# Two DMA queues for the first loads, and another order of VectorE's work at the layers' boundary and at the end of a decoder trunk

## The chip, the cores and the metric

One NeuronCore of a Trainium2 chip runs the whole kernel. The metric is the device time of one execution in microseconds (us). TensorE (PE) multiplies, VectorE (DVE) and ScalarE (ACT) work elementwise, GpSimd (POOL) issues indirect and small transfers, SyncE (SP) issues nearly all the others. Every engine has its own stream of instructions, and they meet at semaphores only.

## The reference

All in float32: SEQ = 512 tokens, D = 1024, two layers.

```python
for l in range(DEPTH):
    mod = silu(c) @ w_ada[l] + b_ada[l]
    sh1, sc1, g1, sh2, sc2, g2 = jnp.split(mod, 6, axis=-1)
    h = modulate(rmsnorm(x, norm1_g[l]), sh1, sc1)
    x = x + g1 * mixer(h, ...)    # projections w_in, retention, pooling, gates, w_out
    h = modulate(rmsnorm(x, norm2_g[l]), sh2, sc2)
    x = x + g2 * moe(h, ...)      # 16 experts, each token goes to two of one group
return rmsnorm(x, final_g)
```

Each expert computes `(silu(x @ w_gate) * (x @ w_up)) @ w_down` for its tokens; the two results of a token are weighted and added.

## The kernel before

The tokens lie in four tiles of 128 rows (t = 0 to 3). A float32 product is made of three passes: each operand is cut into a high part (rounded to fp32r, on ScalarE, names with `_hi`) and the rest (on VectorE, `_lo`), and `three_passes` (L1873 to L1875) multiplies low by high, high by low and high by high. The weights come as pieces of 512 KB through eight slots `raw`, which SP fills in a fixed order; ScalarE makes `w_hi` of a piece, VectorE `w_lo` (L1057 in the mixer, L1602 in the experts), and then the slot is free. The order of the work on each engine is written out by hand.

**The start.** SP loads four x tiles (`x_load`, 512 KB each), then the left column halves of four adaLN pieces (`column_half_load` part 0, 256 KB each, into `raw`), then `first_w` pieces, right halves and more. ScalarE's own queue carries `cond_raw` (4 KB) and, after the sigmoid, `first_rows` (16 KB, biases and norm weights). GpSimd loads `const` (470 KB). ScalarE computes for each x tile the sum of squares (L690) and the deviation (L696), VectorE the reciprocal and `first_normed` (L1148), behind `first_table`, which takes `first_rows` turned by TensorE (L2261, L1093). TensorE multiplies the column halves by the condition (`first_columns`, L2233), then folds, transposes x (L1973) and begins the first products. `keep_busy` (L2003) are matmuls without a use for the result; they read `ones_r`.

**The last expert and the layers' boundary.** Rows that experts 0 to 14 produced are written by indirect transfers into `y_rows` and read back as pairs for each token tile (`pair_early` for t = 0, 1, `pair_2`, `pair_3`; `pairs_load` on SP, L570 to L573). `combine(l, t)` (L1691) adds the pair's two parts, weighted, to x on VectorE, one instruction a part. For t = 2 TensorE does that with diagonal matrices (`pair_matmuls`, L2138). The last expert's rows don't pass through memory: `last_rows_out` (L1633) scales them, `last_rows(l, t)` (L2125) on TensorE spreads them over the tokens of tile t, and `last_add` (L1702) on VectorE adds that to x and raises `x_final`. ScalarE then computes the tile's deviation, VectorE `norm_tile` (h_nat, L1171 and L1173), TensorE `norm_transposes` (L1962), ScalarE hT_hi (L732), VectorE `norm_lo` (hT_lo, L1184), and TensorE takes tile t of group q (`group_tile`, 24 matmuls). The transposed tiles go through two PSUM banks, so a tile's products wait until `norm_lo` has read them (`unit_free`). `last_rows(l, 3)` of layer 0 uses the banks of tile 2 and waits until `last_add(l, 2)` has read them.

**The end.** After the last layer VectorE does combine, `last_add` and `normed_output` (L1711, L1715) tile by tile, and SP stores the tiles (L625, L629). For t = 2 TensorE also adds x itself by an identity matmul (L2389).

**The gate row.** `gate_row` holds g1 or g2, broadcast to all partitions by GpSimd's transfer (L2410); behind the routing VectorE waits for it (L1803) before expert 0. Its first reader is `rows_out(0)` (L1625), in expert 1's turn.

Of the kernel before, what the change touches and what calls it, by code (L numbers as in the profile page):

```python
# [21 lines left out]
ACT = mybir.ActivationFunctionType  # L22
# [3 lines left out]
D = 1024  # L26
T = 512
DEPTH = 2
NT = T // P
# [24 lines left out]
ADA_PIECES = 4  # L54
# [150 lines left out]
def build(nc, w, x_in, c_in, consts, rotary, ada_rows, pool_w, pool_scale, final_g, out):  # L205
# [7 lines left out]
    with ExitStack() as ctx:  # L213
# [59 lines left out]
        squares = sb("squares", [P, D], F32, B)  # L273
# [110 lines left out]
        def k(name):  # L384
            o, n = CONST_AT[name]
            return const[:, o:o + n]
# [149 lines left out]
        def _(sp):  # L536
# [40 lines left out]
                sp.sem_inc(landed[W_SLOTS + j], 16)  # L577
                first_load(PRE + stored_piece(0, W_SLOTS + j), W_SLOTS + j)

            for t in range(NT):  # L580
                x_load(t)
            for j in range(ADA_PIECES):
                column_half_load(2, j, 0, left_landed[j])
            first_w_load(0)
            for j in range(ADA_PIECES):
# [77 lines left out]
        def _(act):  # L663
            act.sem_inc(state_ready, 3)
            act.dma_start(cond_raw[:], c_in).then_inc(c_landed, 16)
            act.wait_ge(c_landed, 16)
            act.activation(cond[:], cond_raw[:], ACT.Sigmoid).then_inc(cond_sig, 1)
            act.dma_start(first_rows[:], ada_rows[0:4].rearrange("a (i p) -> (a i) p", p=P)).then_inc(first_rows_landed, 16)
            act.activation(spare[:], cond_raw[:, 0:1], ACT.Sqrt, scale=0.0)
            act.wait_ge(consts_landed, 16)  # L670
            act.activation(ones_r[:], k("ones"), ACT.Copy).then_inc(ones_ready, 1)

            def hi(l, q, r):
                if l == 0 and q < FIRST_W:
# [13 lines left out]
            def row_deviations(t):  # L688

                act.activation(squares[:], x[:, t], ACT.Square, accum_out=x_ss[:, t:t + 1])  # L690
                act.drain()
                deviation(t)
# [253 lines left out]
            def first_deviation(t):  # L946

                act.wait_ge(x_landed[t], 16)
                row_deviations(t)

            for t in range(NT):
                first_deviation(t)
# [83 lines left out]
        def _(v):  # L1036
# [554 lines left out]
            def expert(l, e):  # L1591
# [29 lines left out]

                def rows_out(before):

                    rows_ready(before)
                    v.tensor_tensor(y_out[:, before % 2].rearrange("p (h n) -> p h n", h=2), ps[:, 2:4],  # L1625
                                    gate_row[:].rearrange("p (h n) -> p h n", h=2), ALU.mult).then_inc(y_copied, 1)
# [10 lines left out]
                if last:  # L1637
                    rows_out(e - 1)
                    lo_e(next(pieces))
                    lo_e(next(pieces))  # L1640
                    last_hot(l)
                    hidden(0)
                    lo_e(next(pieces))
                    hidT(0)
                    if l < DEPTH - 1:
                        for q in range(EARLY):
                            early_low(l + 1, q)
                    lo_e(next(pieces))
                    lo_e(next(pieces))
                    hidden(1)  # L1650
                    lo_e(next(pieces))
                    hidT(1)
                    if l < DEPTH - 1:
                        v.drain().then_inc(raw_used, EARLY)
                    combine(l, 0, [0])
                    last_rows_out()
                    combine(l, 0, [1])
                else:
                    lo_e(next(pieces))
                    lo_e(next(pieces))  # L1660
                    if e == 0:
                        row_numbers(l)
                    if e:
                        rows_out(e - 1)
                    hidden(0)
                    lo_e(next(pieces))
                    lo_e(next(pieces))
                    hidT(0)
                    lo_e(next(pieces))
                    lo_e(next(pieces))  # L1670
                    hidden(1)
                    lo_e(next(pieces))
                    hidT(1)
                    lo_e(next(pieces))
                    lo_e(next(pieces))
                    gathered_lo(E + 1, 1 - odd, [0])
                    lo_e(next(pieces))
                    gathered_lo(E + 1, 1 - odd, [1])
                    for n in pieces:
                        lo_e(n)  # L1680
                    if e == 4:
                        pair_shares()
                    if e == 7:
                        pair_weights()
                    if e == 10:
                        overflow_count()
# [31 lines left out]
            for l in range(DEPTH):  # L1718
# [44 lines left out]
                else:  # L1763
# [2 lines left out]
                    combine(l - 1, 1, [1])  # L1766
                    norm_tile(l, 0, "h1", 0)
                    last_add(l - 1, 1)
                    lo(l, 2, RAW_OF_W[2])
                    norm_lo(l, "h1", 0)  # L1770
                    lo(l, 3, RAW_OF_W[3])
                    norm_tile(l, 0, "h1", 1)
                    last_add(l - 1, 2)
                    norm_lo(l, "h1", 1)
                    combine(l - 1, 3, [0])
                    norm_tile(l, 0, "h1", 2)
                    combine(l - 1, 3, [1])
                    norm_lo(l, "h1", 2)
                    last_add(l - 1, 3)
                    norm_tile(l, 0, "h1", 3)  # L1780
                    norm_lo(l, "h1", 3)
                for q in range(0 if l else W_SLOTS, LAST["O0"] + 1):
# [17 lines left out]
                v.wait_ge(parts_ready, l * 2 + 1)  # L1800
                v.tensor_copy(lg_parts[:, 0:3 * P], ps[:, 7, 0:3 * P]).then_inc(early_parts_copied, 1)
                route_tokens(l)
                v.wait_ge(gate_landed, l * 32 + 32)  # L1803
                for e in range(NE):
                    if e == NE - 1:
                        before, count = overflow_blocks(v, l)
# [61 lines left out]
        def _(pe):  # L1868
# [70 lines left out]
            def group_tile(l, g, t):  # L1939

                for j in range(GROUPS[g][1]):
                    if g == 0 and t == 1 and j == 3:
                        norm_transposes(l, t + 1)
                    if g == NGROUP - 1 and t >= 1 and j == 2:
                        x_transposes(l, t - 1)
                    if g == NGROUP - 1 and t == NT - 1 and j == 3:
                        x_transposes(l, t, [0])
                    product(l, g, j, t)
# [343 lines left out]
            for l in range(DEPTH):  # L2292

                pe.wait_ge(y_copied, l * NE + 1)
                if l:
                    last_rows_pairs(l - 1)
                    norm_transposes(l, 0)
                    last_rows(l - 1, 2)
                    for t in range(NT):
                        pe.wait_ge(unit_free, unit_value(l, "h1", 2 * t + 1) + 2)  # L2300
                        group_tile(l, 0, t)
                        if t == 0:
                            norm_transposes(l, 1)
                            last_rows(l - 1, 3)
                        if t == 2:
                            norm_transposes(l, 3)
                for g in range(1, NGROUP - 1):
                    if ORDER[l][g] == "ap1":
                        pe.wait_ge(norm_pack_landed, l * 16 + 16)
# [39 lines left out]
                with pe.If(count > 0):  # L2349
# [3 lines left out]
                    with pe.Fori(0, count) as slot:  # L2353
# [26 lines left out]
                            mm.then_inc(ov_step, 1)  # L2380
                        pe.wait_ge(ov_pair, b * 80 + 80)
                pe.nop()
                last_rows(l, 0)
                last_rows(l, 1)
                if l == DEPTH - 1:
                    last_rows_pairs(l)
                    pe.wait_ge(x_settled, 1)
                    for half in range(2):
                        pe.matmul(ps[:, ADD_BANK[l][2] + half], ident, x[:, 2, 512 * half:512 * half + 512], start=False, stop=False)  # L2389
                    last_rows(l, 2)  # L2390
                    last_rows(l, 3)
# [223 lines left out]
```

## Time and profile before

| | us |
|---|---|
| median of three runs | 1471.42 |
| lowest and highest | 1470.08, 1474.26 |
| the profiled execution, own time | 1468.83 |
| its span | 1467.2 |
| TensorE busy in it | 1432.4 |
| VectorE busy | 1137.9 |
| ScalarE busy | 775.8 |
| granted clock of TensorE | 0.999 |

The profiled execution is one more run beside the three. Its span is what all rows below refer to; 1.63 us of its own time lie outside the span. Layer 0's mixer begins near 20 us, its experts near 437; layer 1's mixer begins near 742, its experts near 1156. Matmul ends are modelled, so neighbouring matmuls overlap in the rows.

### The profile page before, as it was taken

What the parts mean: (1) busy time and instruction counts of PE and PEld (TensorE: products, weight loads), DVE (VectorE), ACT (ScalarE), POOL (GpSimd) and SP (SyncE); (2) the same over time, 40 slices, a digit from 0 to 9 for tenths busy, and PEclk for the clock granted to TensorE, in tenths of its full rate; (3) what the DMA queues carried; (4) which work ended last, traced back from release to release, by engine and by line L of the source; (5) the groups of instructions that cost most, each with busy time, mean ns of one, the idle gap of its engine ahead of it and who ended that gap; (6) DMA issues with size and microseconds to landing.
All of it is one profiled execution on the core that took longest, in us unless ns stands there. A gap on an engine that the chain in (4) does not pass through costs nothing.

```text
span 1467.2 us, 18889 instructions
## 1 busy us (share of the span) xinstructions
PE 1432.4 (98%) x6815; PEld 1153.5 (79%) x6815; DVE 1137.9 (78%) x1559; ACT 775.8 (53%) x1114; POOL 147.2 (10%) x138
## 2 busy tenths in 40 slices
PE   6999999999999999999989999999999999999997
PEld 4888877878878878888668887878888788888784
DVE  4885786455679999999978557854355899999998
ACT  5524424222348787777633434331233588777773
POOL 0000001000012212111100000100000122112100
PEclk9999999999999999999999999999999999999999
DMA  8766546455567999999945634633254879999995
GB/s 329 282 219 197 185 158 216 154 163 186 174 245 295 393 373 390 383 382 371 361 185 202 201 116 132 206 123 101 76 175 152 320 289 390 376 382 394 367 373 221
DMA packets 108897, 375.39 MB, mean 256 GB/s; under 512 B 16577, under 2 KB 18849, under 8 KB 108160
## 3 DMA queue, kind: packets, MB, share of 16 engines
q1 hardware_dynamic: 92464, 331.39, 62.2%
q0 software_dynamic: 15056, 38.53, 7.3%
q10 hardware_dynamic: 1280, 4.22, 0.9%
q8 instruction: 56, 0.92, 0.2%
q14 instruction: 41, 0.34, 0.1%
HBM read 361.31 MB, written 32.55 MB: 268 GB/s over the span
## 4 chain that ended last, share of the span: by engine, by line
PE 78%; DVE 14%; DMA 3%; ACT 2%; issue 2%; DVEq 1%; ACTq 0%; POOLq 0%; POOL 0%
PE ps L1873 23%; PE ps L1875 23%; PE ps L1874 23%; DVE w_lo L1602 4%; DVE w_lo_more L1602 3%; PE ps L1962 2%; DMA raw<-w 1%; PE ps L2157 1%; DVE y_out L1625 1%; PE ps L2045 1%; PE ps L2206 1%; DVE xgT_lo L1588 1%; ACT w_hi L868 1%; PE ps L2049 1%; ACT w_hi_more L868 1%
## 5 line engine op out<-in xcount | busy, mean ns | idle before, releaser
L1057 DVE TENSOR_TENSOR w_lo<-raw,w_hi 128x1024 fp32r<-128x1024 f32 x130 | 158.9, 1224 | 201.2 <-ACT w_hi L679 199.7
L679 ACT ACTIVATE w_hi<-raw 128x1024 fp32r<-128x1024 f32 x130 | 136.7, 1058 | 324.4 <-PE ps L1875 320.4
L1602 DVE TENSOR_TENSOR w_lo<-raw,w_hi 128x1024 fp32r<-128x1024 f32 x184 | 217.0, 1216 | 2.4 <-DMA gate_row<-mod_rows 1.2
L1602 DVE TENSOR_TENSOR w_lo_more<-raw,w_hi_more 128x1024 fp32r<-128x1024 f32 x176 | 207.6, 1215 | 1.3 <-ACT w_hi_more L868 0.4
L1873 PE MATMUL ps<-w_hi,hT_lo 128*128 128x512 f32 x512 | 204.3, 399 | 2.5 <-DVE hT_lo L1184 2.4
L1875 PE MATMUL ps<-w_hi,hT_hi 128*128 128x512 f32 x512 | 199.8, 390 | 0.0
L1874 PE MATMUL ps<-w_lo,hT_hi 128*128 128x512 f32 x512 | 199.4, 390 | 0.0
L868 ACT ACTIVATE w_hi<-raw 128x1024 fp32r<-128x1024 f32 x184 | 187.7, 1058 | 11.8 <-DMA raw<-w 7.4
L868 ACT ACTIVATE w_hi_more<-raw 128x1024 fp32r<-128x1024 f32 x176 | 179.1, 1057 | 9.4 <-DMA raw<-w 6.8
L1873 PE MATMUL ps<-hT_hi,w_lo 128*128 128x512 f32 x320 | 131.1, 410 | 0.7 <-DVE hT_lo L1153 0.7
L1875 PE MATMUL ps<-hT_hi,w_hi 128*128 128x512 f32 x320 | 125.0, 391 | 0.0
L1874 PE MATMUL ps<-hT_lo,w_hi 128*128 128x512 f32 x320 | 124.8, 390 | 0.0
L1873 PEld LDWEIGHTS ps<-w_hi,hT_lo 128*128 128x128 f32 x512 | 96.1, 188 | 26.2 <-DVE hT_lo L1184 4.6
L1875 PEld LDWEIGHTS ps<-w_hi,hT_hi 128*128 128x128 f32 x512 | 96.1, 188 | 20.7
L1873 PE MATMUL ps<-w_hi,xgT_lo 128*128 128x512 f32 x280 | 111.1, 397 | 0.2 <-DVE w_lo L1602 0.2
L1874 PEld LDWEIGHTS ps<-w_lo,hT_hi 128*128 128x128 f32 x512 | 96.3, 188 | 18.5
L1074 DVE SCALAR_TENSOR_TENSOR ada_acc<-raw,cond,ada_acc 128x512 f32<-128x512 f32 x140 | 104.8, 749 | 6.7 <-issue 0.4
L1875 PE MATMUL ps<-w_hi,xgT_hi 128*128 128x512 f32 x280 | 109.3, 390 | 0.0
L1874 PE MATMUL ps<-w_lo,xgT_hi 128*128 128x512 f32 x280 | 109.2, 390 | 0.0
L2427 POOL DMA_INDIRECT y_rows<-y_out,idx x30 | 65.1, 2171 | 426.8 <-DVE y_out L1625 410.1
L1873 PE MATMUL ps<-w_hi_more,xgT_lo 128*128 128x512 f32 x232 | 91.6, 395 | 0.0
L1875 PE MATMUL ps<-w_hi_more,xgT_hi 128*128 128x512 f32 x232 | 90.5, 390 | 0.0
(306 smaller groups left out, 2641.6 us busy)
## 6 DMA issues: line engine op xcount, KB each, us to landing
raw<-w SPq DMA_DIRECT2D x584, 512.0 KB, 6.1
h_rows<-h POOLq DMA_DIRECT2D x8, 1024.0 KB, 4.9
ahead<-w SPq DMA_DIRECT2D x4, 2048.0 KB, 11.8
y_rows<-x_in ACTq DMA_DIRECT2D x4, 1024.0 KB, 11.6
pair_early<-y_rows SPq DMA_DIRECT2D x4, 1024.0 KB, 6.4
x<-x_in SPq DMA_DIRECT2D x4, 512.0 KB, 6.3
raw<-w SPq DMA_DIRECT2D x8, 256.0 KB, 8.5
first_w<-w SPq DMA_DIRECT2D x4, 512.0 KB, 10.6
```

The costliest lines, as they stand in the source:

```text
L679: act.activation(w_hi[:, q % W_SLOTS], stream_piece(l, q, r), ACT.Copy).then_inc(w_hi_ready, 1)
L868: act.activation(ring_hi(r), expert_piece(e, n), ACT.Copy).then_inc(w_hi_ready, 1)
L1057: v.tensor_tensor(w_lo[:, q % W_SLOTS], stream_piece(l, q, r), w_hi[:, q % W_SLOTS], ALU.subtract).then_inc(raw_used, 1)
L1074: one = v.scalar_tensor_tensor(ada_acc[:, acc], piece, c, ada_acc[:, acc], ALU.mult, ALU.add)
L1588: v.tensor_tensor(xgT_lo[:, slot, cols], ps[:, 4 + j], xgT_hi[:, slot, cols], ALU.subtract).then_inc(xgT_lo_ready, 1)
L1602: v.tensor_tensor(ring_lo(e * EXP + n), expert_piece(e, n), ring_hi(e * EXP + n), ALU.subtract).then_inc(raw_used, 1)
L1625: v.tensor_tensor(y_out[:, before % 2].rearrange("p (h n) -> p h n", h=2), ps[:, 2:4], gate_row[:].rearrange("p (h n) -> p h n", h=2), ALU ...
L1873: pe.matmul(dst, a_lo, b_hi, start=start, stop=False)
L1874: pe.matmul(dst, a_hi, b_lo, start=False, stop=False)
L1875: return pe.matmul(dst, a_hi, b_hi, start=False, stop=stop)
L1962: one = pe.transpose(bank[:, i * P:(i + 1) * P], src[:, i * P:(i + 1) * P], ident)
L2427: pool.indirect_dma_start(y_rows, bass.IndirectOffsetOnAxis(ap=idx[:, e:e + 1], axis=0), y_out[:, e % 2], None, bounds_check=2 * T - 1, oo ...
```

## The change

Half of the first x tiles (t = 1, 3) and half of the left column halves (j = 1, 3) are issued from ScalarE's queue, right behind `cond_raw`. ScalarE waits for `const` after the first tile's squares, and makes `ones_r` after the first deviation. In the last expert both parts of `combine(l, 0)` stand before `last_rows_out`; before, one part stood behind it. At the boundary `norm_lo` of tile 0 goes ahead of `lo(2)`, `combine(3, [0])` ahead of `norm_lo` of tile 1, and `last_add(3)` ahead of `norm_lo` of tile 2; on TensorE the transposes of tile 3 go from behind tile 2's products to before their last quarter. VectorE's wait for `gate_row` goes from before expert 0 to the first reader. At the end of the last layer TensorE waits for `pair_2` and does the first half of its pair matmuls before `last_rows(0)`; the second half stays behind `last_rows(1)`.

```diff
-            for t in range(NT):
+            for t in range(0, NT, 2):
                 x_load(t)
-            for j in range(ADA_PIECES):
+            for j in range(0, ADA_PIECES, 2):
                 column_half_load(2, j, 0, left_landed[j])
...
             act.dma_start(cond_raw[:], c_in).then_inc(c_landed, 16)
+            for t in range(1, NT, 2):
+                act.dma_start(x[:, t], x_in[:, t * D:(t + 1) * D]).then_inc(x_landed[t], 16)
+            for j in range(1, ADA_PIECES, 2):
+                act.dma_start(raw[:, j].rearrange("p (i n) -> p i n", i=2)[:, :, 0:256],
+                              w[bass.ds(ADA_PIECES * 2 + j, 1)].rearrange("o p (i n) -> (o p) i n", i=2)[:, :, 0:256]
+                              ).then_inc(left_landed[j], 16)
             act.wait_ge(c_landed, 16)
             act.activation(cond[:], cond_raw[:], ACT.Sigmoid).then_inc(cond_sig, 1)
             act.dma_start(first_rows[:], ada_rows[0:4].rearrange("a (i p) -> (a i) p", p=P)).then_inc(first_rows_landed, 16)
             act.activation(spare[:], cond_raw[:, 0:1], ACT.Sqrt, scale=0.0)
-            act.wait_ge(consts_landed, 16)
-            act.activation(ones_r[:], k("ones"), ACT.Copy).then_inc(ones_ready, 1)
...
                 act.wait_ge(x_landed[t], 16)
-                row_deviations(t)
+                act.activation(squares[:], x[:, t], ACT.Square, accum_out=x_ss[:, t:t + 1])
+                act.drain()
+                if t == 0:
+                    act.wait_ge(consts_landed, 16)
+                deviation(t)
+                if t == 0:
+                    act.activation(ones_r[:], k("ones"), ACT.Copy).then_inc(ones_ready, 1)
...
                 def rows_out(before):
 
+                    if before == 0:
+                        v.wait_ge(gate_landed, l * 32 + 32)
                     rows_ready(before)
...
-                    combine(l, 0, [0])
+                    combine(l, 0)
                     last_rows_out()
-                    combine(l, 0, [1])
...
                     last_add(l - 1, 1)
+                    norm_lo(l, "h1", 0)
                     lo(l, 2, RAW_OF_W[2])
-                    norm_lo(l, "h1", 0)
                     lo(l, 3, RAW_OF_W[3])
                     norm_tile(l, 0, "h1", 1)
                     last_add(l - 1, 2)
+                    combine(l - 1, 3, [0])
                     norm_lo(l, "h1", 1)
-                    combine(l - 1, 3, [0])
                     norm_tile(l, 0, "h1", 2)
                     combine(l - 1, 3, [1])
+                    last_add(l - 1, 3)
                     norm_lo(l, "h1", 2)
-                    last_add(l - 1, 3)
...
                 route_tokens(l)
-                v.wait_ge(gate_landed, l * 32 + 32)
...
-                    if g == 0 and t == 1 and j == 3:
+                    if g == 0 and t in (1, 2) and j == 3:
                         norm_transposes(l, t + 1)
...
                             last_rows(l - 1, 3)
-                        if t == 2:
-                            norm_transposes(l, 3)
...
+                if l == DEPTH - 1:
+                    pe.wait_ge(pair_in[2], (l + 1) * PAIR_DMAS[2])
+                    pair_matmuls(0)
                 last_rows(l, 0)
                 last_rows(l, 1)
                 if l == DEPTH - 1:
-                    last_rows_pairs(l)
+                    pair_matmuls(1)
                     pe.wait_ge(x_settled, 1)
```

## Rows read from the trace of the kernel before

**Rows 1.** The page: busy us and share by engine; DMA slices.

```profile
...
PE 1432.4 (98%) x6815; PEld 1153.5 (79%) x6815; DVE 1137.9 (78%) x1559; ACT 775.8 (53%) x1114; POOL 147.2 (10%) x138
...
DMA  8766546455567999999945634633254879999995
...
```

**Rows 2.** The chain that ended last, 0 to 20 us: start us, us, what.

```profile
...
5.57 5.39 DMA first_rows<-ada_rows
...
11.10 0.29 PE ps L2261
...
14.71 0.75 DVE x L1148
...
19.73 0.50 PE ps L1873
```

**Rows 3.** Timeline, 0 to 45 us: start, us, instruction, [idle <-releaser].

```profile
...
2.77 2.98 SPq L553 DMA_DIRECT2D raw<-w  x4
...
8.52 0.31 ACT L671 ACTIVATE ones_r<-const 128x128 fp32r<-128x128 f32 x1 [1.08 <-DMA const<-consts]
...
13.53 0.19 PEld L2233 LDWEIGHTS ps<-raw,cond_wide 128*32 128x32 f32 x4 [0.56 <-DMA raw<-w]
...
14.15 0.29 ACT L696 ACTIVATE x_std<-x_ss,const 128x1 f32<-128x1 f32 x1
...
```

**Rows 4.** Windows: stretch, busy by engine, PEclk, DMA share, GB/s.

```profile
...
3.00:4.00 1.00, 0.00 (x0) 0.00 (x0) 0.00 (x0) 0.00 (x0) 0.00 (x0) 1.00 0.69 197
4.00:5.00 1.00, 0.00 (x0) 0.00 (x0) 0.00 (x0) 0.00 (x0) 0.00 (x0) 1.00 0.93 319
...
12.00:13.00 1.00, 1.00 (x9) 0.38 (x8) 0.92 (x3) 0.93 (x4) 0.00 (x0) 1.00 1.14 393
...
```

**Rows 5.** Timeline of VectorE, 720 to 772 us, the layers' boundary.

```profile
...
726.18 1.28 DVE L1691 SCALAR_TENSOR_TENSOR x<-pair_early,w_early,x 128x1024 f32<-128x1024 f32 x1 [0.51 <-DMA pair_early<-y_rows]
728.85 1.29 DVE L1633 TENSOR_TENSOR y_out<-ps,gate_row 128x512 f32<-128x512 f32 x2 [1.39 <-PE ps L1875]
...
731.99 1.28 DVE L1691 SCALAR_TENSOR_TENSOR x<-pair_early,w_early,x 128x1024 f32<-128x1024 f32 x1 [0.66 <-issue]
...
741.23 1.28 DVE L1184 TENSOR_TENSOR hT_lo<-ps,hT_hi 128x512 fp32r<-128x512 f32 x2
...
```

**Rows 6.** Timeline of TensorE, 720 to 772 us, the layers' boundary.

```profile
...
739.10 1.09 PE L1962 MATMUL ps<-const,h_nat 128*128 128x128 f32 x8 [2.31 <-DVE h_nat L1173]
...
742.57 0.50 PE L1873 MATMUL ps<-w_hi,hT_lo 128*128 128x512 f32 x1 [0.65 <-DVE hT_lo L1184]
...
757.58 0.51 PE L1873 MATMUL ps<-w_hi,hT_lo 128*128 128x512 f32 x1 [0.18 <-DVE hT_lo L1184]
...
763.18 1.09 PE L1962 MATMUL ps<-const,h_nat 128*128 128x128 f32 x8
765.85 0.50 PE L1873 MATMUL ps<-w_hi,hT_lo 128*128 128x512 f32 x1 [1.57 <-DVE hT_lo L1184]
...
```

**Rows 7.** Timeline, all engines, 1156 to 1178 us, first expert of layer 1.

```profile
...
1161.73 2.36 DVE L1602 TENSOR_TENSOR w_lo<-raw,w_hi 128x1024 fp32r<-128x1024 f32 x2 [1.15 <-DMA gate_row<-mod_rows]
...
1163.01 0.51 PE L1873 MATMUL ps<-w_hi,xgT_lo 128*128 128x512 f32 x1 [0.23 <-DVE w_lo L1602]
...
1172.80 1.09 PE L2157 MATMUL ps<-const,xg 128*128 128x128 f32 x8 [0.61 <-DMA xg<-h_rows,idx]
...
```

**Rows 8.** Timeline, all engines, 1446 to 1468 us, the end.

```profile
...
1447.24 3.67 PE L2125 MATMUL ps<-y_out,slot_last 128*128 128x512 f32 x8 [0.87 <-DVE y_out L1633]
...
1455.90 3.60 PE L2125 MATMUL ps<-y_out,slot_last 128*128 128x512 f32 x8
...
1460.15 1.22 DVE L1702 TENSOR_TENSOR x<-ps,x 128x1024 f32<-128x1024 f32 x1
...
```

**Rows 9.** DMA issues near 1439.03 us, SP: KB each, us to landing.

```profile
...
pair<-y_rows SPq DMA_DIRECT2D x1, 1024.0 KB, 10.6
```


## The prediction

> **What bounds the kernel now.** I read the page's busy shares first, then the slices, then the chain and timelines of the three places that the diff touches. TensorE is busy for 98% of the span and its slices are full from the second one on [rows 1]. So time can only be won or lost where TensorE waits or idles: in the first 20 us, at the layers' boundary and behind the last expert. In the experts VectorE and the DMA engines are full as well, so there a stall of VectorE counts. I look at four places.
>
> **Start, before.** The chain of the first 20 us doesn't run over the x tiles. It runs over first_rows, a small load on ScalarE's queue, issued at 5.57 and landed at about 11.0 [rows 2]. TensorE's first transpose (11.10) and VectorE's first_turned wait for it, the four first_normed tiles stand behind that on VectorE (the last starts at 14.71), and then come first_part, the fold, first_scale, w_lo and hT_lo up to the first product at 19.73. Everything from 11.10 to 19.73 hangs on this landing, 8.6 us behind it. ScalarE's statistics run beside it: the fourth deviation starts at 14.15 and ends 0.29 later, just in time for the last first_normed [rows 2, 3]. The two chains are equally long, so shortening one alone wins nothing.
>
> **Start, after.** The diff puts two x tiles (2 x 512 KB) and two column halves (2 x 256 KB) on ScalarE's queue ahead of first_rows. Before, first_rows was issued when all four halves were already out (SP's four issues end at 5.75) and still landed at 11.0, ahead of the last half, for which TensorE waited until 13.53 [rows 2, 3]. It could overtake since it stood in another queue. After, it stands in the same queue behind 1.5 MB. The other half of the work, also 1.5 MB, is on SP's queue, and the bandwidth is used up: 319 GB/s in the microsecond from 4 on and 393 in that from 12 [rows 4]. So I expect the halves to land about when they do now and first_rows with the last of them. What two queues may win is the low rate of the first microseconds: 197 GB/s in the one from 3 to 4 us [rows 4], and about as little in the one before; filling two or three such slices up to 400 would bring some 0.4 MB, 1.0 us at the rate of later. That leaves 12.4 to 13.4 for the landing. I take 12.9, nearer to the end that the rows show: 1.9 us later than now. Bounds: 0 (it lands as now, at 11.0) and, if SP's first_w piece (512 KB, 1.3 us at 393) also goes ahead, +3.7. The move of consts_landed lets ScalarE begin its squares before const has landed; its deviations come about 1.0 us earlier (it waited 1.08 for const before ones_r, whose 0.31 us now stand between tile 0 and 1) [rows 3]. That is hidden: VectorE waits for first_rows. ones_r itself is wanted only by keep_busy behind the columns at about 14.5. The four issues on ScalarE (at most 0.75 us each, as SP's halves [rows 3]) are over by about 4 us, and it waits for c_in until it issues first_rows at 5.57 [rows 2]: nothing. **Start: +1.9.**
>
> Here the Trainium skill bears, DMA: Bandwidth & Descriptors, "Queues, rings and completion order": engines alternate between queues packet by packet, and one queue's descriptors are consumed in order. The overtaking above agrees with the first part (11.0 against 13.4); no run here yet shows the second for a long queue. By it first_rows can't pass the halves in its own queue, so 13.4 and +2.4 would be the value, against 0 if order did not matter.
>
> **Boundary, tile 0.** Last expert of layer 0: both halves of combine(0) now go before last_rows_out. VectorE started the first at 726.18, so two of them (2 x 1.3 us) just end when the y_out multiplication starts at 728.85, and that is not delayed [rows 5]. Behind it one combine (1.3) is gone: the next combine starts at about 730.9 instead of 731.99, 1.1 earlier [rows 5]. It, last_add(0), ScalarE's squares and norm_tile(0) follow at unchanged distances, so norm_transposes(0) go from 739.10 to 738.0 [rows 6]. Now the order: before, norm_lo(0) stood behind lo(2) and started at 741.23, and the tile's product at 742.57 [rows 5, 6]. After, norm_lo(0) can run as soon as ScalarE's hT_hi is there. For tile 3 that order stood already: 2.67 us from the start of the transposes at 763.18 to the product at 765.85 [rows 6]. So here 738.0 + 2.6 = 740.6. TensorE itself is through its transposes and last_rows(2) (0.9 + 1.8) at 740.7. So the product starts at 740.7: 1.9 earlier. lo(2) now ends at 741.7; its piece is needed 12 matmuls (2.7 us) into the tile, at 743.4. Hidden by those; if it stood another 1.7 later it would not be.
>
> **Boundary, tiles 1 to 3.** Walking on with 5.5 us a tile (24 matmuls; tile 2 took 5.6 from 757.58 to 763.18), 0.9 for eight transposes, 1.8 for one last_rows (half of 3.60) [rows 6, 8] and VectorE's durations of before: VectorE's norm_tile(1) ends at 745.5, tile 0 ends at 746.2, last_rows(3) at 748.9. norm_lo(1) now stands behind combine(3,[0]) and ends at 749.3: tile 1 starts at 749.3, about 1.4 earlier, some of the lead gone. Tile 2 starts at 756.1 by the same steps, against 757.58 [rows 6]. Then the moved transposes: before, norm_transposes(3) came behind tile 2 at 763.18, and TensorE waited for hT_lo until 765.85, 2.67 us with 0.9 of work in them [rows 6]. After, they stand before the last quarter of tile 2, at 756.1 + 4.1 = 760.2. Is h ready? last_add(3) is moved ahead of norm_lo(2) and ends at 754.8, ScalarE's deviation at 756.6 (squares start behind hT_hi at 755.2), norm_tile(3) takes 2.8: 759.6. Yes, with 0.6 to spare. hT_lo is there at 760.2 + 2.7 = 762.9, TensorE's own work ends at 762.5. Tile 3 starts at 762.9 instead of 765.85 [rows 6]: **boundary −2.9**, −2 if the 0.6 and the distances of norm_lo(2) don't hold, −3.4 if TensorE doesn't wait at tile 3. All that comes later is started by TensorE's and VectorE's own progress, so it moves along.
>
> **The gate wait.** In layer 1 VectorE stood 1.15 us for gate_row before expert 0's w_lo at 1161.73. Behind it TensorE waited at 1163.01 (0.23) and, because the row numbers and so the gathers were late, at 1172.80 (0.61) [rows 7]. gate_row is read first by expert 1's turn, some 20 us on, so the new wait costs nothing. In layer 0 no such wait stands: 0. **−0.8**, the sum of TensorE's two waits; bounds 0 and −1.15.
>
> **The end.** pair_matmuls(0) now go before last_rows(0), with a wait for pair_2. TensorE was idle for 0.87 us before last_rows at 1447.24, but pair_2 was issued at 1439.03 and landed 10.6 later, at 1449.6 [rows 8, 9]. So TensorE, and last_rows(0) and (1) behind it, stand until 1449.6, where they now have been under way for 2.4 us. TensorE's whole work there, in whatever order, took from 1447.24 to 1459.5, when the eight records of last_rows(2) and (3) from 1455.90 were done [rows 8]: 12.3 us. From 1449.6 this ends at 1461.9. VectorE's last_add(3) needs it and was at 1460.15, 0.65 behind it [rows 8]. It goes to about 1462.0. VectorE's own path, with both combines ahead, is 0.25 late at y_out and 0.9 early behind it; that gain is gone in the wait. **End +1.8**; bounds +1.2 (pair_2 half a microsecond earlier) and −0.8 (pair_2 there in time, the gain of the combine alone).
>
> **Sum.** +1.9 − 2.9 − 0.8 + 1.8 = 0.0. The profiled execution took 1468.83 (span 1467.2), the median of the runs is 1471.42, 2.6 above it; I add the sum to the median: 1471.4.
>
> **Rivals.**
> A: neither transfer is late. ScalarE's queue, having long x packets while SP's has its short halves, drains first and first_rows lands by 11.1; pair_2 comes in time. Then 0 − 2.9 − 0.8 − 0.8 = −4.5: 1466.9. For it: the idle rate before 4 us. Against it: 10.6 us for pair_2, and 1.5 MB can't pass in half the bandwidth by 11.1. pair_2 in time alone gives 1.9 − 2.9 − 0.8 − 0.8 = −2.6: 1468.8.
> B, the slower side: the loads of both queues are taken in the order of issue. SP's issues now run ahead of first_rows (issued at 5.57), with first_w and up to four right halves: 1.5 MB, 3.9 us at 393 GB/s [rows 4]. Then it lands at 17.3, start +6.3, in all +4.4: 1475.8. Only from a landing at 17.3 on would it be slower by more than a measurement tells; from 13 on it is slower at all. For it: first_rows took 5.4 us for 16 KB [rows 2]. Against it: it did overtake the last halves.
> C: at the boundary only tile 0's gain stays (norm_tile(3) late, TensorE waits as before): −1.5, in all +1.4: 1472.8.
> D: spreading the issues changes nothing at all, neither the order nor the landing: 0 − 2.9 − 0.8 + 1.8 = −1.9: 1469.5. The Trainium skill says so on the same page, "Issuing engines are not separate DMA queues": loads from several engines only save issue time. The rows give SP's last half issue an end at 5.75 and a landing at 13.4 [rows 3].
>
> **Numbers.** My forecast 0.42, A in full 0.08 and pair_2 alone 0.15, B 0.08, C 0.12, D 0.15. What a measurement can tell from no change is 0.3%, 4.4 us. Nearly every case lies within that; A in full and B stand on its edges, and the DMA-bound experts may shift a microsecond or two either way. Faster by over 0.3%: 0.14; within: 0.76; slower: 0.10. Range 1467 to 1475.3: A and B end just outside.
>
> **What would show it.** Right: first_rows lands at 12.4 to 13.5 and the first product starts at 21 to 22.5; the product of tile 3 starts 34 us behind last_rows_out instead of 37; no gate_row wait in layer 1; at the end TensorE waits for pair_2 before L2138's matmuls and last_add(3) waits for TensorE. Wrong: first_rows at 11, no wait for pair_2, or a wait for h_nat inside tile 2. Work in the experts that stretches by more than 1 us would be outside my steps.

## The result, and the profile after

The changed kernel takes 1475.84 us (median of 19 runs, 1472.99 to 1478.84), the kernel before on the same chip 1470.08 (19 runs, 1467.73 to 1474.26). The ratio is 1.0036, with a 95% interval of 1.003 to 1.0043: slower, where no change was forecast, and just outside the range (1467 to 1475.3). The profiled executions have spans of 1473.6 and 1467.2 us, 6.4 apart.

**Start.** The chain that ended last, of the changed kernel, 0 to 24 us (start us, us, what):

```profile
...
6.28 9.78 DMA first_rows<-ada_rows
...
16.19 0.30 PE ps L2271
...
19.81 0.75 DVE x L1158
...
```

And its timeline there:

```profile
...
23.00 2.85 PE L2013 MATMUL ps<-ones_r 128*128 128x512 f32 x6
...
23.37 1.55 DVE L1163 SCALAR_TENSOR_TENSOR hT_lo<-ps,first_cols,hT_hi 128x512 fp32r<-128x512 f32 x2
...
25.69 0.40 PE L1883 MATMUL ps<-hT_hi,w_lo 128*128 128x512 f32 x1
...
```

Its DMA issues of 0 to 45 us (out<-in, queue, count, KB each, median us from issue to landing):

```profile
...
x<-x_in SPq DMA_DIRECT2D x2, 512.0 KB, 6.3
x<-x_in ACTq DMA_DIRECT2D x2, 512.0 KB, 9.4
raw<-w ACTq DMA_DIRECT2D x2, 256.0 KB, 11.8
...
first_rows<-ada_rows ACTq DMA_DIRECT2D x1, 16.0 KB, 9.8
```

And its windows for the first microseconds (stretch, busy by engine, PEclk, DMA share, GB/s):

```profile
...
2.00:6.00 4.00, 0.00 (x0) 0.00 (x0) 0.50 (x4) 1.28 (x1) 0.16 (x1) 1.00 0.77 195
...
```

The chain is still the one over first_rows [rows 2], but the 16 KB now take 9.8 us instead of 5.4 and are issued 0.7 later, since cond_raw, ahead of them, also landed later. Everything behind the landing hangs on it, as before: the last first_normed starts at 19.81 (14.71 before), the first product at 25.69 (19.73). Before, the four microseconds from 2 to 6 moved 297 GB/s (197 and 319 are two of them [rows 4]); now 195. TensorE's work stands 6.0 us later at the first product, 5.9 at 507 us and 5.7 from 609 us on.

**Boundary.** TensorE of the changed kernel, 722 to 772 us (start, us, instruction, [idle <-releaser]):

```profile
...
728.50 0.50 PE L1883 MATMUL ps<-w_hi_more,hidT_lo 128*128 128x512 f32 x1 [0.82 <-DVE w_lo_more L1612]
...
736.31 3.67 PE L2135 MATMUL ps<-y_out,slot_last 128*128 128x512 f32 x8 [1.78 <-DVE y_out L1645]
...
755.41 0.50 PE L1883 MATMUL ps<-w_hi,hT_lo 128*128 128x512 f32 x1 [0.35 <-DVE hT_lo L1194]
...
762.22 0.50 PE L1883 MATMUL ps<-w_hi,hT_lo 128*128 128x512 f32 x1 [0.20 <-DVE hT_lo L1194]
...
766.44 1.04 PE L1972 MATMUL ps<-const,h_nat 128*128 128x128 f32 x8
...
769.05 0.50 PE L1883 MATMUL ps<-w_hi,hT_lo 128*128 128x512 f32 x1 [0.19 <-DVE hT_lo L1194]
...
```

The first of these matmuls, still the last expert's, started at 722.78 before:

```profile
...
722.78 0.50 PE L1873 MATMUL ps<-w_hi_more,hidT_lo 128*128 128x512 f32 x1 [0.84 <-DVE w_lo_more L1602]
...
```

Tile 3 starts at 769.05 instead of 765.85 [rows 6], so 5.72 us of lateness have become 3.20: the boundary gave back 2.5. The transposes stand inside tile 2 (766.44) without a wait, and the wait at tile 3 is 0.19 instead of 1.57. A loss is in this number. Ahead of y_out VectorE's moved combine waited for pair_early:

```profile
...
732.66 2.66 DVE L1702 SCALAR_TENSOR_TENSOR x<-pair_early,w_early,x 128x1024 f32<-128x1024 f32 x2 [1.28 <-DMA pair_early<-y_rows]
735.47 1.29 DVE L1645 TENSOR_TENSOR y_out<-ps,gate_row 128x512 f32<-128x512 f32 x2
...
```

y_out and TensorE's last_rows(0) start 6.62 us later than before (735.47 against 728.85 [rows 5]), 0.9 more than the lateness ahead of them. From y_out on the new order gives 3.4: tile 3 starts 33.6 us behind it instead of 37.0.

**Gate wait.** No wait for gate_row stands in layer 1. The first matmul of expert 0 is 3.21 us late (1159.48 against 1156.27), the transposes for expert 2 are 2.41 late (1193.17 against 1190.76): −0.8. At TensorE's last expert matmul it is 2.46 (1448.44 against 1445.98).

**End.** All engines of the changed kernel, 1448 to 1474 us:

```profile
...
1452.72 3.52 PE L2148 MATMUL ps<-pair,diag_w 128*128 128x512 f32 x4 [3.89 <-DMA pair<-y_rows]
...
1456.07 3.60 PE L2135 MATMUL ps<-y_out,slot_last 128*128 128x512 f32 x8
...
1459.51 1.88 PE L2148 MATMUL ps<-pair,diag_w 128*128 128x512 f32 x4
...
1466.58 1.23 DVE L1713 TENSOR_TENSOR x<-ps,x 128x1024 f32<-128x1024 f32 x1 [0.65 <-PE ps L2135]
...
```

Its windows there:

```profile
...
1450.00:1452.00 2.00, 0.00 (x0) 0.00 (x0) 1.86 (x4) 0.00 (x0) 0.00 (x0) 1.00 1.02 412
1452.00:1454.00 2.00, 1.28 (x2) 0.77 (x3) 1.92 (x2) 0.00 (x0) 0.00 (x0) 0.61 0.43 174
1454.00:1456.00 2.00, 2.00 (x3) 0.75 (x3) 0.26 (x1) 0.00 (x0) 0.00 (x0) 0.54 0.02 8
1456.00:1458.00 2.00, 2.00 (x6) 0.95 (x5) 0.01 (x1) 0.00 (x0) 0.00 (x0) 1.00 0.00 0
```

TensorE does nothing for 3.89 us and then runs four pair matmuls in 3.52 us; the same four take 1.88 at 1459.51. The granted clock of those windows is 0.61 and 0.54, nearly all of it the lower level (1.2 GHz). last_add(3) starts at 1466.58, 6.4 later than before [rows 8], and 2.4 to 2.5 of that were there already: the end has added 4.0. The sum, from the 5.7 that are left of the start's 6.0 at 722 us: +5.7 − 2.5 − 0.8 + 4.0 = +6.4, the whole difference of the spans.

### The profile page after: what moved, and what is told of

The parts are those of the page before. It is cut to its first block, busy times and chain, and to the rows that moved or that the text cites. A ratio compares the mean times of both kernels' runs of the same rounds, so it can differ in the third digit from the quotient of the medians.

```text
span 1473.6 us, 18887 instructions
## 1 busy us (share of the span) xinstructions
PE 1433.6 (97%) x6815; PEld 1155.7 (78%) x6815; DVE 1138.6 (77%) x1559; ACT 774.9 (53%) x1114; POOL 154.2 (10%) x138
## 4 chain that ended last, share of the span: by engine, by line
PE 83%; DVE 10%; DMA 3%; ACT 2%; issue 1%; DVEq 1%; SPq 0%; ACTq 0%; POOLq 0%
PE ps L1883 24%; PE ps L1885 24%; PE ps L1884 24%; DVE w_lo L1612 3%; DVE w_lo_more L1612 2%; PE ps L1972 2%; PE ps L2167 1%; PE ps L2114 1%; PE ps L2216 1%; PE ps L2055 1%; DMA y_rows<-y_out,idx 1%; DVE xgT_lo L1598 1%; DVE y_out L1637 1%; ACT w_hi L872 1%; PE ps L2059 1%
## 5 line engine op out<-in xcount | busy, mean ns | idle before, releaser
L1883 PEld LDWEIGHTS ps<-w_hi,hT_lo 128*128 128x128 f32 x512 | 96.2, 188 | 24.8 <-DVE hT_lo L1194 3.1
L2438 POOL DMA_INDIRECT y_rows<-y_out,idx x30 | 69.7, 2322 | 421.3 <-DVE y_out L1637 404.6
```

The lines of the kernel that those rows point to most:

```text
L1883: pe.matmul(dst, a_lo, b_hi, start=start, stop=False)
L2438: pool.indirect_dma_start(y_rows, bass.IndirectOffsetOnAxis(ap=idx[:, e:e + 1], axis=0), y_out[:, e % 2], None, bounds_check=2 * T - 1, oo ...
```

## The experiments

The four parts (start, boundary, gate wait, end) can be undone one by one, so that each can be priced alone. Two questions then stay for each of the two losses. At the start: does first_rows land late because it stands behind the tiles in its own queue, because SP's later loads take bandwidth, or because two queues make the first microseconds slow? At the end: is it the wait alone, or the clock behind it too? In each group of kernels that ran on one chip, the kernel before had a median between 1469.8 and 1470.6. Single executions differ by 1 to 2 us in the experts, so where a kernel was executed only once, the start of a named instruction is compared and not the total.

**1. The start's edits alone, and all but them.** The first kernel is the one before plus this; the second is the changed one without it.

```
 act.dma_start(cond_raw[:], c_in)
+for t in (1, 3): x tile t on ScalarE's queue    (SP: tiles 0, 2)
+for j in (1, 3): column half j on ScalarE's queue (SP: halves 0, 2)
 ...
-act.wait_ge(consts_landed, 16); ones_r
+the same two behind tile 0's squares and deviation
```

> The kernel before with the start's edits alone. Theory Q (first_rows stands on ScalarE's queue behind two x tiles and two halves, and SP's queue, whose issues run ahead, takes more than half of the bandwidth): first_rows lands at about 16 us instead of 11.0, the products of layer 0 start 5.9 us late, and this is carried to the end: +5.9 us against before, ratio 1.004. Rival S (the 5.9 us are an accident of one profiled execution, or are partly won back in the rest of the kernel): clearly under +4 us.

> The changed kernel with the loads, the wait for const and ones_r of the start as before. Theory Q: first_rows lands at 11.0 again, so -5.9 us against the changed kernel: what is left is boundary -2.7, gate wait -0.8, end +4.0, in sum +0.5 us against before. Rival S: more than +2 us against before is left.

Alone, the start costs 1475.41 against 1470.57 (ratio 1.0032, 1.002 to 1.0044); first_rows reaches TensorE at 16.21 and the first product starts at 25.73, 6.0 later than before. Without it, the changed kernel takes 1469.87 (0.9992, 0.9983 to 1.0002), first_rows lands as before (11.06), and tile 3 of the boundary starts at 762.83. Both agree: the start's edits alone cost what makes the change slower. In the medians it is 4.8 us, where 5.9 was expected. What first_rows standing behind the loads of its own queue costs is shown more cleanly by kernel B of experiment 4.

The second one also keeps the end, and shows its price again (its chip, all engines, 1440 us to the end):

```profile
...
1445.83 3.78 PE L2138 MATMUL ps<-pair,diag_w 128*128 128x512 f32 x4 [3.17 <-DMA pair<-y_rows]
1449.41 4.89 PE L2125 MATMUL ps<-y_out,slot_last 128*128 128x512 f32 x8
...
```

**2. first_rows ahead of the tiles in the same queue** (the changed kernel, with its issue moved right behind cond_raw's).

```
 act.dma_start(cond_raw[:], c_in)
+act.dma_start(first_rows[:], ...)
 for t in (1, 3): ...
```

> The changed kernel with first_rows issued right behind cond_raw, ahead of the four loads on ScalarE's queue; all else as changed. Theory Q: first_rows lands by about 7 us and nothing waits for it; then the last column half binds (15.6 us in the changed kernel against 13.3 before), so the first product starts about 1 us later than before, not 6: about -4.9 us against the changed kernel. Rival R (the start is late since three queues together move less in the first microseconds, whoever's load comes first): the late halves keep the start at +3 us or more against before.

It takes 1471.60 (1.0004, 0.9995 to 1.0013), 4 us less than the changed kernel. So its late issue behind 1.5 MB is what makes first_rows late; whether by the queue's order or by the 4.8 us that the issue comes later (6.28 against 1.43) this kernel alone doesn't tell. But the start isn't as before: now TensorE waits for the column halves. Timeline of 0 to 30 us of this kernel:

```profile
...
9.53 0.31 PE L2271 MATMUL ps<-const,first_rows 32*128 32x32 f32 x1 [9.53 <-DMA const<-consts]
12.42 1.07 PE L2243 MATMUL ps<-raw,cond_wide 128*32 128x256 f32 x4 [2.58 <-DMA raw<-w]
13.97 1.08 PE L2243 MATMUL ps<-raw,cond_wide 128*32 128x256 f32 x8 [0.48 <-DMA raw<-w]
16.22 1.07 PE L2243 MATMUL ps<-raw,cond_wide 128*32 128x256 f32 x4 [1.16 <-DMA raw<-w]
...
```

The last half is there at 16.2, where it was at 13.53 [rows 3], and the first product starts at 22.20, 2.5 later than before and not 1. Only 211 GB/s were moved from 2 to 6 us. The split loads themselves are late.

**3. SP holds its next load back** until a half of ScalarE's queue has landed (the changed kernel).

```
+sp.wait_ge(left_landed[1], 16)
 first_w_load(0)
```

> The changed kernel, but SP waits until the first column half of ScalarE's queue (j = 1) has landed before it issues first_w and all that follows; only the landings are of interest, the weights behind come late. Theory Q2 (part of the lateness of first_rows is that SP's later loads take bandwidth while ScalarE's queue still holds the halves): the last half and first_rows land 1.5 us or more earlier than the 15.6 and 16.1 of the changed kernel, near 14. Rival R (only the slow first microseconds, 195 GB/s from 2 to 6 us against 297 before, and the queue's own order count): first_rows stays within 0.5 us of 16.1. The whole kernel is slower than the changed one, since first_w then lands behind 17 us.

first_rows reaches TensorE at 14.60, 1.6 earlier than in the changed kernel: SP's later loads do take their share from ScalarE's queue. The first product starts at 23.72, 2.0 earlier, and the one execution takes 1472.39. I had expected the kernel as a whole to get slower since first_w would be late; it didn't, because first_rows was what the start waited for.

**4. Only the tiles split, and only the halves split.** Both keep first_rows behind the loads of its queue.

```
 kernel A: x tiles 1, 3 on ScalarE's queue; all four halves on SP's
 kernel B: all four x tiles on SP's; halves 1, 3 on ScalarE's queue
```

> The changed kernel with all four column halves on SP's queue again; only x tiles 1 and 3 are issued from ScalarE's, ahead of first_rows. Theory T (the slow first microseconds, 195 GB/s from 2 to 6 us against 297 before, come from x tiles begun on two queues at once beside const): about 200 GB/s again from 2 to 6 us. first_rows now has 1 MB ahead of it and lands near 12 to 13. Rival H (the halves with their 1 KB rows on ScalarE's queue make the first microseconds slow): 280 GB/s or more.

> The changed kernel with all four x tiles on SP's queue again; only column halves 1 and 3 are issued from ScalarE's, ahead of first_rows. Theory T: 280 GB/s or more from 2 to 6 us, since one queue alone carries the x tiles. If the engines take the queues in turn packet by packet, these halves come in beside the x tiles, early, and the x tiles later; first_rows, with 0.5 MB ahead of it, lands by 11 to 12. Rival H: about 200 GB/s from 2 to 6 us.

The windows of A, then of B:

```profile
...
2.00:6.00 4.00, 0.00 (x0) 0.00 (x0) 0.51 (x4) 1.28 (x1) 0.16 (x1) 1.00 0.86 196
...
4.00:5.00 1.00, 0.00 (x0) 0.00 (x0) 0.00 (x0) 0.00 (x0) 0.00 (x0) 1.00 0.62 141
...
```

```profile
...
2.00:6.00 4.00, 0.00 (x0) 0.00 (x0) 0.60 (x4) 1.50 (x3) 0.16 (x1) 1.00 0.90 290
...
4.00:5.00 1.00, 0.00 (x0) 0.00 (x0) 0.00 (x0) 0.09 (x1) 0.00 (x0) 1.00 0.95 323
...
```

The low rate comes with the x tiles on two queues (196 GB/s) and not with the halves (290, as the 297 of before). Idle DMA engines explain only a part: from 4 to 5 us they are busy for 0.62 of the time in A, but from 2 to 6 us for 0.86, nearly the 0.90 of B, and still move a third less. In A first_rows reaches TensorE at 12.64, as expected. In B it does so at 13.60, where I expected 11 to 12. B is the cleaner comparison for the queue's order: first_rows is issued when it was before (5.61, 5.57), the rate is nearly the same, and two halves stand in its own queue instead of SP's. It is 2.5 us later (11.10 to 13.60), and TensorE then finds all halves landed, where before it waited for the last until 13.53: it no longer comes ahead of them. One more thing differs: SP, with two issues fewer, sends its first_w at 4.59 instead of 5.80, so what SP's later loads take isn't parted from the 2.5. Both totals, 1471.37 and 1472.35, lie between the kernel before (1470.03) and the changed one.

**5. The end's order undone** (the changed kernel, TensorE's work behind the last expert as before; the combine on VectorE stays moved).

```
-pe.wait_ge(pair_in[2], ...); pair_matmuls(0)
 last_rows(l, 0); last_rows(l, 1)
-pair_matmuls(1)
+last_rows_pairs(l)
```

> The changed kernel with TensorE's order at the end as before (both pair matmuls behind last_rows(0) and (1)); both combines stay ahead of last_rows_out. Theory P (TensorE stands for pair_2, then runs the next matmuls at half clock, and last_add(3) waits for it): the end goes from +4.0 to about -0.5 us against before, so -4.5 us against the changed kernel, and no granted clock under 1 behind the last expert. Rival C (the end is late since both combines now stand ahead of last_rows_out and wait for pair_early): the end stays over +1.5 us.

It takes 1470.91 (1.0006, 0.9996 to 1.0016), 4.9 less than the changed kernel. The stretch from the last expert matmul to the end of the span is 20.7 us, against 24.8 in the changed kernel and 20.8 before. The moved combine wins next to nothing there:

```profile
...
1446.00 2.66 DVE L1702 SCALAR_TENSOR_TENSOR x<-pair_early,w_early,x 128x1024 f32<-128x1024 f32 x2 [0.84 <-DMA pair_early<-y_rows]
...
1461.93 1.23 DVE L1713 TENSOR_TENSOR x<-ps,x 128x1024 f32<-128x1024 f32 x1 [1.27 <-PE ps L2135]
...
```

It waits for pair_early, and last_add(3) waits for TensorE (1.27). In the first kernel of experiment 7, with the same order at the end, it waits for only 0.16 us, and the stretch is 20.2: then the combine wins 0.6.

**6. TensorE kept busy while it waits for pair_2.** Fourteen matmuls of ones, whose result nobody reads, stand ahead of the wait; the rest is the changed kernel.

```
+for _ in range(14): pe.matmul(ps[:, 6], ones_r, ones_r)
 pe.wait_ge(pair_in[2], ...)
 pair_matmuls(0)
```

> The changed kernel with 14 extra matmuls without use (ones into a free PSUM bank, 0.23 us each, 3.2 us) on TensorE behind the last expert, ahead of its wait for pair_2. It fills the idle time of 3.9 us that the wait makes. Theory K (the four pair matmuls behind the wait took 3.52 us instead of 1.88 since the granted clock had fallen after the idle time): they take 1.9 us again, no stretch under 1.0 clock, and the end is 1.6 us earlier: about -1.6 us against the changed kernel, +4.2 against before. Rival (the records are slow for another reason, such as reading pair_2 while the DMA engines still write): they stay over 3 us, no change.

```profile
...
1447.21 3.33 PE L2018 MATMUL ps<-ones_r 128*128 128x512 f32 x14
...
1451.35 1.98 PE L2153 MATMUL ps<-pair,diag_w 128*128 128x512 f32 x4 [0.81 <-DMA pair<-y_rows]
1453.17 3.60 PE L2140 MATMUL ps<-y_out,slot_last 128*128 128x512 f32 x8
...
```

The four pair matmuls take 1.98 us instead of 3.52, and the granted clock is 1.00 in every window there. So the 3.52 are the clock, and the clock fell because TensorE did nothing. The kernel takes 1472.32 (1.0011, 1.0001 to 1.0021). Each against the kernel before on its own chip, that is +2.6, and the changed kernel +5.8: 3.2 less, where I expected 1.6. The profiled spans differ by 2.9, and the rows place it: 1.4 behind the last expert matmul (23.3 instead of 24.8), 0.9 at the boundary's last_rows(0), whose wait is 0.88 instead of 1.78, and 0.5 at the first product (25.18). The last two aren't this edit's.

**7. Boundary and gate wait alone** (start as before, TensorE's order at the end as before), **and the same with first_rows issued first** and const's wait moved, all loads on SP's queue.

> The changed kernel without the start's edits and with TensorE's order at the end as before: what is left is the boundary, the gate wait and both combines ahead. Theory by steps: boundary -2.7 to -2.9, gate -0.8, combine at the end -0.1, in all -3.7 us against before, ratio 0.9975. Rival G (what is won at the boundary is given back in the experts, which DMA and VectorE bound): within 1.5 us of before.

> Boundary, gate wait and combines as changed, TensorE's order at the end as before, all loads on SP as before, but first_rows issued right behind cond_raw on ScalarE's queue and the later wait for const kept. Theory Q: first_rows lands by 7 us, VectorE's four first_normed are done about 1 us earlier by ScalarE's earlier statistics, then the last column half (13.3) binds and first_part starts at about 14.8 instead of 15.4: start -0.6 us, in all -4.3 us against before, ratio 0.9971. Rival: first_rows first delays the x tiles and nothing is won over the kernel with the old start.

The first takes 1465.36 (1464.21 to 1466.84) against 1469.77: 0.9966, 0.9954 to 0.9978, faster than both kernels: −4.4, where −3.7 was expected, so the boundary's gain isn't given back in the experts. In its trace the last tile starts at 762.32:

```profile
...
755.48 0.50 PE L1873 MATMUL ps<-w_hi,hT_lo 128*128 128x512 f32 x1 [0.19 <-DVE hT_lo L1184]
...
762.32 0.50 PE L1873 MATMUL ps<-w_hi,hT_lo 128*128 128x512 f32 x1 [0.20 <-DVE hT_lo L1184]
...
```

The second takes 1465.82 (0.997, 0.9959 to 0.998). first_rows, issued at 1.44, takes 5.2 us and is no longer what the start waits for: TensorE's transpose of it waits for const until 8.69, then the column halves bind (the last until 13.61), and the first product starts at 18.83 instead of 19.49. The halves stood close behind first_rows, so no more than that is won, and the 0.7 can't be seen in the total.

**8. The moved transposes alone.** The first kernel of 7 with norm_transposes(3) back behind tile 2.

```
-if g == 0 and t in (1, 2) and j == 3: norm_transposes(l, t + 1)
+if g == 0 and t == 1 and j == 3: norm_transposes(l, t + 1)
 ...
+if t == 2: norm_transposes(l, 3)
```

> The kernel boundary_gate with norm_transposes(3) behind tile 2's products as before. It prices this one move: TensorE waits for hT_lo of tile 3 again, some 1.6 us, and starts tile 3 at 1.5 us more behind last_rows(0) than boundary_gate does. Rival: VectorE's order alone brings tile 3 forward, and the move is worth under 0.5 us.

```profile
...
730.21 5.37 PE L2125 MATMUL ps<-y_out,slot_last 128*128 128x512 f32 x8 [1.95 <-DVE y_out L1635]
...
757.00 0.50 PE L1873 MATMUL ps<-w_hi,hT_lo 128*128 128x512 f32 x1 [0.19 <-DVE hT_lo L1184]
762.58 1.03 PE L1962 MATMUL ps<-const,h_nat 128*128 128x128 f32 x8
765.18 0.50 PE L1873 MATMUL ps<-w_hi,hT_lo 128*128 128x512 f32 x1 [1.57 <-DVE hT_lo L1184]
```

From tile 2 to tile 3 it takes 8.18 us, against 6.84 (755.48 to 762.32) with the move: 1.3 of the boundary's 3.4 is the transposes', where 1.5 was expected, and the rest VectorE's order. The wait of 1.57 is back, the number of before [rows 6]. This execution also had a long wait at last_rows(0) (1.95) and 5.37 us for eight matmuls that otherwise take 3.67, with granted clocks of 0.88 and 0.50 in the windows of 2 us from 730 and 732 on. It is the clock of experiment 6 at another place, which is why I compare distances within the tiles and not its total (1467.79).

## Why the prediction was wrong

**Start: the step that failed.** The prediction says "That leaves 12.4 to 13.4 for the landing. I take 12.9", and counts the 8.6 us from there to the first product as before: +1.9. Measured: it landed at 16.1, and the first product came 6.0 later. The mechanism, a small load caught behind the loads of its own queue, was right (experiments 2 and 4); the size was off. The split was priced as a gain of up to 1.0 us, by filling the slow microseconds; in fact it made them slower, 195 GB/s instead of 297 over 4 us, 0.4 MB less, and experiment 4 puts that on the x tiles. The halves were taken to land "about when they do now", where experiment 2 has the last at 16.2 instead of 13.5. And SP's later loads were left to the upper bound (+3.7), where experiment 3 shows that they cost 1.6. Of the 5.1 us that first_rows is late at TensorE (11.10 to 16.19), an account is: 2.5 by its own queue's order (kernel B of experiment 4), 1.6 by SP's loads (experiment 3), and about 1.0 by the 0.4 MB at 393 GB/s, which is worked out. The parts come from different kernels and may overlap, so that they add up proves little.

Another 0.9 came behind the landing: from there to the first product it took 9.5 us instead of 8.6. Before, the first product waited for hT_lo and started with its end, and the six keep_busy matmuls were long over:

```profile
...
17.41 1.62 PE L2003 MATMUL ps<-ones_r 128*128 128x512 f32 x6
...
```

In the changed kernel hT_lo is done at 24.92, but the product stands behind the keep_busy matmuls in TensorE's own stream, and they take 2.85 us instead of 1.62; it starts at 25.69, 0.8 behind hT_lo. Kernel B of experiment 4 shows the same (hT_lo done at 22.33, product at 23.12). That is 0.47 us a matmul, where the same ones took 0.24 in experiment 6. It looks like the lower clock, but the granted clock reads 1.00 in these windows, so that isn't shown.

Rival B named nearly this size (landing at 17.3, in all 1475.8) by another mechanism, that loads of both queues are taken in the order of issue. Experiments 2 and 3 don't speak against it, but kernel A of experiment 4 does: there first_rows (12.64) lands ahead of two halves that were issued before it on SP's queue (TensorE waits for them until 13.75 and 14.50), as it did in the kernel before. By what shares the engines divide themselves between the two queues stays open. Rival D, that spreading the issues changes nothing, is out by 5 us at the start. It goes with the Trainium skill's DMA: Bandwidth & Descriptors, "Issuing engines are not separate DMA queues", which says that several issuing engines only save issue time; this case's runs don't agree, as the same 16 KB reach TensorE 2.5 us later with two halves moved into their queue (kernel B), and the rate of the first microseconds moves from 297 to 195 GB/s in the changed kernel. The same page's "Queues, rings and completion order", by which one queue's descriptors are taken in order, agrees with kernel B (13.60); for the changed kernel the landing "with the halves", 13.4, was only a lower bound.

**Boundary: mechanism right, and the net number right by luck.** −2.9 was forecast, −2.5 measured in the changed kernel. That is two misses against each other. The new order itself gives −3.4, in the changed kernel from y_out on as in the first kernel of experiment 7 (tile 3 33.6 us behind y_out in both, where the prediction said 34). There tiles 1, 2 and 3 start at 748.65, 755.48 and 762.32, and the walk had 749.3, 756.1 and 762.9: its steps from tile to tile held, and the 0.6 stood already at the first transposes (737.30, forecast 738.0). What the walk left out is the wait for pair_early ahead of y_out (1.28), which costs 0.9. It isn't simply a matter of being late: the kernel of experiment 5, 5.4 us late there, waits 0.23, and that of experiment 8, 0.5 us early, waits 1.43. What sets it stays open.

**Gate wait: right.** −0.8 forecast, −0.8 measured.

**End: mechanism right, size off.** TensorE stands for pair_2, as forecast, and last_add(3) waits for TensorE. +1.8 was forecast, +4.0 measured. The prediction's step "From 1449.6 this ends at 1461.9" took all of TensorE's 12.3 us at the high level. It had been idle for 3.89 us, and four matmuls then ran at the low one: +1.6, which experiment 6 takes away. The other 0.6 is pair_2 itself: issue to landing takes 11.1 us instead of 10.6, and it lands 3.9 behind TensorE's last expert matmul instead of 3.3. The combine's gain was taken as lost in the wait for TensorE, and in the changed kernel last_add(3) does start with the end of TensorE's work.

**The total.** With these two sizes as measured and the rest as forecast the sum of the prediction would be +6.0 − 2.9 − 0.8 + 4.0 = +6.3, against +5.8 in the medians. The chance of 0.10 for "slower" hung almost wholly on the queue order of rival B (0.08). That the two losses that were already in the sum could both be two or three times as large wasn't priced at all. And the 0.3% taken as the least that a measurement can tell was too much: 19 runs of each kernel leave 0.07% either side.

## What to carry to other kernels

A second DMA queue doesn't add bandwidth here: before moving large loads to it, look which small load is issued behind them, and let it be issued first. If an engine's wait is moved ahead of its other work, price the clock of the work behind the wait too, not only the wait. Matmuls that only keep TensorE busy stand ahead of real work as well (0.8 us at the start here, when they ran slowly). And take the edits apart: here the two that cost (start and end) hid 4.4 us that the other two win.

## What the runs showed of the hardware

- x tiles of 512 KB begun from two queues: 194 to 211 GB/s from 2 to 6 us in each of the seven kernels that did so, against 285 to 297 in the six with all tiles on one queue. A part is DMA engines that stand idle (share 0.47 from 4 to 5 us in the changed kernel, 0.93 before [rows 4]), and a part that they move less while busy (195 GB/s at a share of 0.77 from 2 to 6 us, 297 at 0.90). It was seen each time and not explained.
- TensorE's granted clock fell from 1.00 to the lower level (1.2 GHz) behind idle stretches of 3.89, 3.17 and once of 1.95 us, and four matmuls of 128x512 took 3.52 and 3.78 us instead of 1.88. With 0.81 us of idle time it stayed at 1.00, and with 1.78 at the place where the 1.95 stood. Beyond that, the same length went both ways: the 2.31 us ahead of the first transposes of the boundary [rows 6] left it at 1.00, while the 2.32 at the same place with the start's edits alone were followed by 0.57, and four matmuls took 3.23 us.
- A transfer of 16 KB took 5.4 us from issue to landing with only cond_raw ahead of it in its queue, 6.1 behind two tiles, 7.9 behind two halves, 9.8 behind both, and 8.1 behind both with the other queue held back. More in front of it in bytes isn't always later: the two tiles are twice the two halves.
